# VectorE makes the first gated half and its turned low part earlier in the last expert tile

## The reference

```python
def hierarchical_moe(x, wg, bg, we, be, w_gate, w_up, w_down):
    ...
    for e in range(N_EXPERTS):                       # 16 experts, each token uses 2
        h = jax.nn.silu(xt @ w_gate[e]) * (xt @ w_up[e])   # the gated hidden row, 512 wide
        y = y + combine[:, e:e + 1] * (h @ w_down[e])
    return y.reshape(b, s, d)
# afterwards: rms_norm(x + y, final_norm_g)
```

## Time and profile before

| | |
|---|---|
| median of 3 runs | 788.7 us (787.71 to 789.83) |
| the profiled execution's own time | 789.02 us |
| its span | 787.3 us |
| mean granted TensorE clock | 0.996 |
| PE busy | 764.9 us (97%) |
| DVE busy | 492.3 us (63%) |
| ACT busy | 450.5 us (57%) |
| POOL busy | 209.3 us (27%) |

### The profile page before, as it was taken

How to read it: one execution, slowest core, us unless ns; L and a number is a source line. 1 busy time by engine, 2 the same in 40 slices (tenths; PEclk the granted TensorE clock), 3 DMA queues, 4 the chain that set the end, 5 groups by cost and what they waited for, 6 DMA issues and landing times.

```text
span 787.3 us, 10839 instructions
## 1 busy us (share of the span) xinstructions
PE 764.9 (97%) x3739; PEld 621.8 (79%) x3739; DVE 492.3 (63%) x702; ACT 450.5 (57%) x590; POOL 209.3 (27%) x124
## 2 busy tenths in 40 slices
PE   7999999999999999999999999999999999999994
PEld 4788777777787888888888788878778888888782
DVE  5704476585743302322022669999999998999888
ACT  5244657566744232323321556787878888888862
POOL 3644433232332444434442532000000000000033
PEclk9999999999999999999999999999999999999998
DMA  8569999792222262332328438999999999999965
GB/s 300 183 213 381 370 337 393 268 342 75 69 66 81 81 214 87 100 107 81 107 97 282 161 131 285 408 409 409 409 409 409 410 409 410 409 409 341 398 251 202
DMA packets 134318, 206.74 MB, mean 263 GB/s; under 512 B 10813, under 2 KB 65669, under 8 KB 134278
## 3 DMA queue, kind: packets, MB, share of 16 engines
q1 hardware_dynamic: 126084, 188.80, 65.7%
q10 hardware_dynamic: 5890, 9.04, 3.1%
q0 software_dynamic: 2304, 8.39, 2.8%
HBM read 157.95 MB, written 48.25 MB: 262 GB/s over the span
## 4 chain that ended last, share of the span: by engine, by line
PE 85%; DVE 6%; ACTq 2%; DMA 2%; POOL 2%; ACT 1%; issue 1%; DVEq 0%; SPq 0%; POOLq 0%
PE ps L1052 25%; PE ps L1054 24%; PE ps L1053 24%; DVE w_lo L389 3%; PE ps L1342 2%; PE ps L1146 1%; PE ps L1174 1%; PE ps L1157 1%; PE ps L1295 1%; POOL raw_mg L656 1%; PE ps L1269 1%; DMA x<-in_x 1%; PE ps L1349 1%; ACTq L877 1%; DMA raw_mg<-slots,slot_idx 1%
## 5 line engine op out<-in xcount | busy, mean ns | idle before, releaser
L383 POOL TENSOR_TENSOR w_lo<-raw,w_hi 128x1024 fp32r<-128x1024 f32 x72 | 174.1, 2422 | 250.4 <-ACT w_hi L371 250.4
L371 ACT ACTIVATE w_hi<-raw 128x1024 fp32r<-128x1024 f32 x73 | 76.8, 1057 | 195.4 <-PE ps L1054 168.0
L1052 PE MATMUL ps<-xn_hi,w_hi 128*128 128x512 f32 x352 | 140.6, 399 | 0.0
L1054 PE MATMUL ps<-xn_hi,w_lo 128*128 128x512 f32 x352 | 137.2, 390 | 0.0
L1053 PE MATMUL ps<-xn_lo,w_hi 128*128 128x512 f32 x352 | 137.1, 390 | 0.0
L1052 PE MATMUL ps<-w_hi,xT_hi 128*128 128x512 f32 (+1 forms) x248 | 97.0, 391 | 2.2 <-DVE w_lo L389 2.2
L1054 PE MATMUL ps<-w_hi,xT_lo 128*128 128x512 f32 (+1 forms) x248 | 95.1, 384 | 0.0
L1053 PE MATMUL ps<-w_lo,xT_hi 128*128 128x512 f32 (+1 forms) x248 | 94.9, 383 | 0.0
L656 POOL DMA_INDIRECT raw_mg<-slots,slot_idx x7 | 7.8, 1113 | 280.4 <-DMA slots<-y_tile 278.5
L1052 PEld LDWEIGHTS ps<-xn_hi,w_hi 128*128 128x128 f32 x352 | 66.1, 188 | 16.2 <-issue 2.0
L1053 PEld LDWEIGHTS ps<-xn_lo,w_hi 128*128 128x128 f32 x352 | 66.1, 188 | 14.1 <-issue 1.0
(11 more groups left out here) (311 smaller groups left out, 1475.1 us busy)
## 6 DMA issues: line engine op xcount, KB each, us to landing
slots<-raw SPq DMA_DIRECT2D x65, 512.0 KB, 7.0
raw<-in_w_in SPq DMA_DIRECT2D x52, 512.0 KB, 4.0
raw_mg<-in_exp_w_down SPq DMA_DIRECT2D x35, 512.0 KB, 11.0
raw<-in_exp_w_gate SPq DMA_DIRECT2D x29, 512.0 KB, 11.3
raw_a<-in_exp_w_gate SPq DMA_DIRECT2D x26, 512.0 KB, 10.6
raw_c<-in_exp_w_up SPq DMA_DIRECT2D x24, 512.0 KB, 11.8
raw_mg<-in_exp_w_up SPq DMA_DIRECT2D x22, 512.0 KB, 11.9
raw<-in_exp_w_up SPq DMA_DIRECT2D x15, 512.0 KB, 11.8
```

What stands on the lines that cost most here:

```text
L371: nc.scalar.activation(w_hi[:, b % HI_SLOTS, :], raw_buf(b), ACT.Copy)\
L383: eng.tensor_tensor(w_lo[:, b % HI_SLOTS, :], raw_buf(b), w_hi[:, b % HI_SLOTS, :].bitcast(F32), ALU.subtract)\
L1052: pe.matmul(dst, hi_l, hi_r, start=start, stop=False)
L1054: return pe.matmul(dst, lo_l, hi_r, start=False, stop=stop)
```

## The change

In the last tile's loop on DVE, step 9 now makes the gated half 0 before the low part of block 12, and step 10 the turned low part of half 0 before the low part of block 13. The gated half 1 stays behind block 13's low part.

```diff
             for s in range(PER_TILE + 1):
                 if s == PER_TILE:
                     hT_lo_half(1)
-                split_lo_loop(at, s + AHEAD)
                 if s == 9:
                     dve.wait_ge(S["hT_ps"], at.i)
                     dve.wait_ge(S["silu_done"], tiles)
                     hidden_half(0)
                 if s == 10:
                     hT_lo_half(0)
+                split_lo_loop(at, s + AHEAD)
+                if s == 10:
                     hidden_half(1)
```

## The result

The changed kernel takes 790.1 us (22 runs, 788.64 to 791.47), the one before 788.75 us (22 runs on the same chip, 787.42 to 790.36). The ratio is 1.0016, 95% interval 1.001 to 1.0022: slower by 1.3 us. That is less than the 0.3% that the prediction took as the least a measurement can tell, but the interval does not include 1, so with 22 runs each the loss is clear. The time lies at the upper end of the stated range (787.2 to 790.4) and outside of what the forecast alone gave (788.4 to 789.3, middle 788.9).

The account below looks back on a forecast made before the run. The prediction took gather 7's landing to bound the end: 789.02 - 0.86 (PE's wait) + 0.86 (DVE waits longer) + 0.2 (later landing) = 789.2 us, or 788.9 as the profiled execution lies 0.3 above the median; range 787.2 to 790.4.

Parts of the forecast that it names:

- PE's wait goes, 0.86 us, and nothing else is late on PE: Last tile, turning of half 0: it starts 0.86 us earlier; half 1 gated has the smallest margin, 0.3 us.
- None of it reaches the end, because `first_sum(3)` waits for gather 7: At the sums: of PE's 0.86 us, 0 remains; DVE's idle before `first_sum(3)` grows from 0.58 to as much as 1.4.
- The rival that PE's gain reaches the end: Gathers do not bound the end; gain up to 0.86 us, middle 788.1 us; chance 0.13.
- Gathers are blocked by DVE's two-input instructions: POOL's gather issues last longer by the rest of DVE's instruction less 0.05 us; gather 7's issue ends 1.21 us later.
- How much of the later issue reaches the landing: Gather 7's landing: +0.2 us taken, between bounds of 0 (backlog hides all) and +1.21 (landing follows issue).
- The rival "the landing follows the issue": Gather 7's data finds the DMA engines empty: slower by 0.6 to 1.2 us, say 789.7 us; chance 0.20.
- the prediction's own signs: In the changed profile: `first_sum(3)` at 772.3 to 773.2; forecast wrong if before 772.2 or moved by the issue's full delay.
- the backlog term: DMA engines are behind, 3.9 gathers moved when six were issued, so the late gather 7 issue costs only +0.2 us.
- The row of 5.76 us: Gather 7 from issue at 766.81 to landing at 772.57, read as set by the queue; one gather needs 1.51 us.
- The "last 16.4 us" behind the gather: Stretch from `first_sum(3)` at 772.59 to the end at 789.02, said to hang on the seventh gather.

Follow-up runs that it names:

- Experiment 5: Changed kernel with only 32 of 1024 columns of the low parts of blocks 12 to 15 made on VectorE; 789.42 us against 788.49 for the kernel before.
- 7: Changed kernel with the low parts of blocks 12 to 15 and the first sums each made by two 512-column instructions; 790.64 us against 788.49 before.
- experiment 6: Kernel before the change with a 128x1024 memset on GpSimd between gathers 6 and 7; 789.43 us against 788.49.
- 11: Changed kernel with `first_sum(1)` behind instead of ahead of the second half of the last rows' low part; 789.74 us against 788.71 before.
- 4: Changed kernel with first choices of token groups 2 and 3 gathered fourth and sixth; 789.59 us against 789.07 for the kernel before.
- 8: Kernel before the change with first choices of token groups 2 and 3 gathered fourth and sixth; 788.84 us against 788.49.
- 1: Changed kernel with half 0's turned low part back behind block 13's low part, so only the gated half moves; 789.39 us against 789.07 before.
- 12: Kernel before with only gated half 0 moved up and first choices of groups 2 and 3 gathered fourth and sixth; 788.49 us against 788.71.
- 2: Changed kernel with gated half 0 back behind block 12's low part, so only the turned low part moves; 789.04 us against 789.07 before.
- 3: Kernel before the change with one small 128x1 GpSimd addition between the issues of gathers 4 and 5; 788.91 us against 789.07.

## Why the prediction came out as it did

- **PE's wait goes, 0.86 us, and nothing else is late on PE.** Right: the turning of half 0 comes 0.87 earlier against the mark, that of half 1 0.91.
- **None of it reaches the end, because `first_sum(3)` waits for gather 7.** Right, in both traces of the changed kernel. The rival that PE's gain reaches the end is out. What the prediction did not see is a wait ahead of it: DVE's idle time was to grow to over 1 us in front of `first_sum(3)`, and it is 0.31 and 0.73 there, because `first_sum(2)` already stands 2.00 and 1.79 us for the fifth gather, whose issue is 1.0 us later.
- **Gathers are blocked by DVE's two-input instructions.** Right, nearly to the digit (of the eight old issues four were blocked, not all, as one sentence of the prediction reads). Predicted excess for gathers 2 to 7: 0.18, 0.51, 0.24, 0.31, 0, 0.83; measured over 0.94: 0.19, 0.43, 0.22, 0.33, 0, 0.83. Start of gather 7, against the mark: predicted 10.97, measured 10.91. Experiment 5 took the blocking work away and the excess went; in 7 each block ended with the half instruction it had met.
- **How much of the later issue reaches the landing: I took +0.2 of 1.21.** This is the term that was mis-sized. The two traces show +0.9 for an issue 1.15 later and +1.2 for one 1.25 later. The rival "the landing follows the issue" (0.20) is what happened, at 790.1 against its 789.7. By the prediction's own signs the backlog term failed: `first_sum(3)` was to start at 772.3 to 773.2, and on that clock it starts at 773.5 and 773.8. That the measured time lies in the stated range is due to the width that the rivals and the scatter of single runs gave it, not to this term. I had divided the total of moved bytes by the size of a gather and found a reserve of 0.2 to 0.6 gathers at each arrival. That count assumed that the DMA engines go on at their old rate as long as anything is issued; they fell to 279 GB/s while 1.2 to 2.4 gathers were issued and not yet moved. Whether single ones of the 16 had run out of work or the transfers themselves were slower is open. The row of 5.76 us, which I took for a queue, is about the same for a seventh gather that is issued late: over 0.83 later, landed 0.78 later (experiment 6).
- The traces point to two sources that overlap. The seventh's late issue alone costs 0.78 (6); the late issues of gathers 2 to 5, with the seventh's own at 0.94 and over 0.32 later than before, cost 0.73 to 0.77 (11, `first_sum(3)` at 17.14 against 16.37 and 16.41). Together 0.9 to 1.2. Each rests on one trace, and the pair of experiments 4 and 8 shows that the price depends on more than the issue times: with the same delays the seventh landing moved by 0.1 us there.
- **A side count.** The "last 16.4 us" behind the gather took the end from the execution's time and the start from the span's clock; within the span of 787.3 us it is 14.7. The forecast does not use it.
- **Not settled.** The medians lie above what the traced tails say for five kernels (1, 4, 5, 8 and 12 show shorter tails than before, by 0.1 to 0.7 us, and no shorter time). For two of them I compared the spans of all runs, and they side with the times: the median span of experiment 5 is 787.45 us against 786.6 for before, that of experiment 8 787.05 against 786.6. So the difference lies inside the program, in tails that were not traced or ahead of the mark. One trace for each is too little to say which, and it also leaves open whether all of the 1.3 us is in the tail.

## What to carry to other kernels

Where a chain ends in transfers that POOL issues, an edit on VectorE is also an edit of the issue times: put both engines' timelines side by side and work out which issues will meet which VectorE instructions. A backlog counted as moved bytes over the whole stretch is no sure cover for a late issue: here the same delay of 1.15 us moved the seventh landing by 0.9 us in one order of the gathers and by 0.1 us in another, so let the range reach to the full delay. Idle time removed from an engine that the last chain doesn't pass was worth nothing here, however plain the wait looked in the timeline.

## What the runs showed of the hardware

- The issue of one of these indirect DMAs took GpSimd 0.93 to 0.96 us when VectorE was running nothing with two SBUF inputs, and up to 1.89 us otherwise (experiment 11, the eighth). The excess over 0.94 is what is left of the VectorE instruction that was already running, up to its recorded end, less 0.08 to 0.14 us (nothing where less than 0.1 us was left), for 128x1024 instructions and those of 512 columns alike. In the traces VectorE's instructions keep their usual durations meanwhile (1.22 us for a low part): POOL is the one that waits.
- The first gather started 1.90 or 1.91 us after the mark and took 1.31 or 1.32 us in all fourteen traces, although it is released by the landing of a store: it starts beside the low part of block 11, whose end sets its own, and so the whole row of issues was in step with VectorE each time.
- Landing minus end of issue for the seventh gather: 4.8 and 4.9 us in the two traces before, 4.6 and 4.8 in the two after, 4.7 to 5.1 in experiments 1 to 3, 4.8 with the memset ahead of it, 5.2 and 5.3 in experiments 7 and 11, and 4.0 and 5.1 in experiments 4 and 8. Before and experiment 8 have the same issue times and differ by 0.2, so that much is scatter or the order of the gathers.
